# Both score banks awaited first, all four cross scores at once, and a re-ordered router in a two-layer decoder trunk

## What is computed

```python
def nsa(q, k, v):                     # 8 query heads, 2 key heads; two of its three branches are dense here
    s = q @ k.T * scale + t5_bias     # per head and branch: 256 tokens x 256 keys, causal
    return masked_softmax(s) @ v
...
def cross_attention(hn, memn, ...):   # 4 heads of 64
    s = jnp.einsum('bshd,bmhd->bhsm', q, k) * HEAD_DIM ** -0.5
    p = jax.nn.softmax(s, axis=-1)
    return jnp.einsum('bhsm,bmhd->bshd', p, v).reshape(bsz, seq, X_WIDTH) @ w_o
...
def moe_swiglu(x2, w_router, w_up, w_down):
    logits = x2 @ w_router
    top_val, top_idx = lax.top_k(logits, 2)
    gate = jax.nn.softmax(top_val, axis=-1)
    # each expert: gather its tokens, swiglu, times gate, add back
```

## Time and profile before

| what | value |
|---|---|
| time, median of 3 runs | 1373.01 us (1373.0 to 1373.81) |
| the profiled execution: its time | 1374.09 us |
| its span, first to last instruction | 1372.3 us |
| PE busy (x instructions) | 1310.5 us, 96% (x21428) |
| DVE busy | 636.4 us, 46% (x1404) |
| ACT busy | 425.5 us, 31% (x847) |
| mean granted clock of TensorE | 0.976 |
| experts, from their first up product to the end | 717.48 us to 1372.3 us |

### The profile page before, as it was taken

One profiled execution on the slowest core, in us unless ns is written; L12 is line 12 of the kernel. 1 busy time (PEld: TensorE's weight loads), 2 busy tenths in 40 slices (PEclk: granted clock), 3 DMA queues, 4 the chain that ended last, 5 costly groups with the idle time before them and its releaser, 6 DMA issues.

```text
span 1372.3 us, 48306 instructions
## 1 busy us (share of the span) xinstructions
PE 1310.5 (96%) x21428; PEld 1079.5 (79%) x21428; DVE 636.4 (46%) x1404; ACT 425.5 (31%) x847; POOL 89.8 (7%) x139
## 2 busy tenths in 40 slices
PE   7998897999999999989789999999999999999998
PEld 5855555777777685554659999999999999999997
DVE  7876313103322237651245555555555555455554
ACT  4425413001002122541313333343333333333332
POOL 0450100000000017000100000000000000000000
PEclk9997899999999999999889999999999999999999
DMA  8530043244241054102649999999999999999990
GB/s 351 211 123 1 1 184 122 90 171 184 104 172 62 34 240 154 63 1 90 248 175 390 426 426 427 426 427 426 426 426 427 427 426 426 427 426 426 426 403 33
DMA packets 32865, 357.68 MB, mean 261 GB/s; under 512 B 3715, under 2 KB 5379, under 8 KB 6700
## 3 DMA queue, kind: packets, MB, share of 16 engines
q1 hardware_dynamic: 30656, 353.78, 62.4%
q10 hardware_dynamic: 2156, 3.18, 0.7%
HBM read 355.88 MB, written 1.06 MB: 260 GB/s over the span
## 4 chain that ended last, share of the span: by engine, by line
PE 88%; DVE 5%; ACT 3%; issue 2%; DMA 1%; POOL 1%; ACTq 0%; POOLq 0%; DVEq 0%
PE bank L2102 29%; PE bank L1556 26%; PE bank L2118 14%; PE bank L2049 6%; PE bank L2164 2%; PE bank L2089 2%; PE bank L1564 1%; PE bank L1829 1%; PE bank L1706 1%; PE bank L1576 1%; PE bank L1894 1%; ACT ring L575 1%; DVE ring L968 1%; PE bank L1650 1%; PE bank L2002 0%
## 5 line engine op out<-in xcount | busy, mean ns | idle before, releaser
L2102 PE MATMUL bank<-R,ring 128*64 128x80 f32 x11264 | 421.7, 233 | 0.7 <-DVEq L950 0.7
L2102 PEld LDWEIGHTS bank<-R,ring 128*64 128x64 f32 x11264 | 403.0, 137 | 8.3 <-issue 8.3
L1556 PE MATMUL bank<-ring 128*128 128x256 f32 (+1 forms) x1408 | 368.4, 421 | 8.6 <-DVE ring L968 4.9
L1556 PEld LDWEIGHTS bank<-ring 128*128 128x128 f32 x1408 | 269.4, 193 | 106.2 <-issue 67.3
L841 ACT ACTIVATE ring<-ring 128x1024 f32<-128x1024 f32 x176 | 186.0, 1057 | 146.7 <-PE bank L2118 146.7
L2118 PE MATMUL bank<-zz,ring 128*64 128x80 f32 x5632 | 224.8, 233 | 0.0
L2118 PEld LDWEIGHTS bank<-zz,ring 128*64 128x64 f32 x5632 | 207.9, 137 | 0.0
L1518 DVE SCALAR_TENSOR_TENSOR zz<-zz,bank 128x80 f32<-128x80 f32 x176 | 41.9, 238 | 198.8 <-PE bank L2102 198.3
L1497 DVE COPY ring<-ring 128x1024 f32<-128x1024 f32 x177 | 121.6, 687 | 1.9 <-DVE R L1487 1.9
L1501 DVE COPY ring<-ring 128x1024 f32<-128x1024 f32 x177 | 121.5, 686 | 0.1
L837 ACT ACTIVATE X<-bank 128x80 f32<-128x80 f32 x176 | 41.7, 237 | 246.1 <-PE bank L2102 246.1
(11 more groups left out here) (299 smaller groups left out, 1029.4 us busy)
## 6 DMA issues: line engine op xcount, KB each, us to landing
ring<-moe_w_dram SPq DMA_DIRECT2D x177, 1536.0 KB, 10.7
ring<-ffn_w_dram SPq DMA_DIRECT2D x11, 3072.0 KB, 10.2
ring<-w_in_dram SPq DMA_DIRECT2D x6, 2048.0 KB, 10.4
ring<-w_out_dram SPq DMA_DIRECT2D x4, 2048.0 KB, 8.5
ring<-w_x_dram SPq DMA_DIRECT2D x2, 3072.0 KB, 10.6
ring<-w_small_dram SPq DMA_DIRECT2D x2, 2896.0 KB, 10.1
ring<-w_in_dram SPq DMA_DIRECT2D x2, 2144.0 KB, 21.0
ring<-bias_rows_dram ACTq DMA_DIRECT2D x1, 1536.0 KB, 11.1
```

The lines of the kernel that those rows point to most:

```text
L1556: i = pe.matmul(out_ap, a, b, start=(k == 0), stop=(k == n - 1))
L2102: e = pe.matmul(pb[out_bank][c0:c0 + 64, 0:CAP], half[:, P * k + c0:P * k + c0 + 64], xg[:, k], start=(k == 0), stop=(k == KT - 1), tile_p ...
```

## The change

Four things, all ahead of the experts. `scores(p)` opens both banks and then makes both products. The cross scores of units 0 to 3 go to banks 6, 7, 4 and 3 and are all made ahead of the first transposes; each unit has its own column of `nmx`, and DVE takes the four maxima without waiting for exponentials in between. In the router, the clearing of `table` and `zeros` stands ahead of the wait for the constants; the copies of the gates into `table` and the first step of `pos` stand ahead of the wait for `count`; the flag and the release of two banks (`overflow`) stand behind `pick(0)`. No instruction is added or left out.

```diff
@@ -44,6 +44,7 @@
 HEADS = [0, 4, 1, 5, 2, 6, 3, 7]
 SLOTS = 4
 BU_BANKS = [3, 4, 7, 1, 3, 4, 7, 3]
+XS_BANKS = [6, 7, 4, 3]
 S5_AT = [dict(bu0=4, bu4=7, bu6=9, ys0=10), dict(bu0=3, bu4=6, bu6=9, ys0=9)]
 UPW, DNW = KT * 2 * 256, 2 * D
 FF_SLOTS = [2, 3, 1, 0, 2, 3, 1, 0, 2, 3, 1]
@@ -213,7 +214,7 @@
             a(f"cross_T{g}_", g % 2)
         a("xq", 2, 2); a("xqT_", 3)
         for u in range(4):
-            a(f"xs{u}_", 6 + u % 2, 0)
+            a(f"xs{u}_", XS_BANKS[u], 0)
             a(f"xpT{u}_", u % 2)
         a("xo0_", 2); a("xo1_", 5); a("xoT", 3)
         for g in range(4):
@@ -570,10 +571,10 @@
                 act.activation(R[:, 0], turn_rows, ACT.Sin,
                                scale=-2 * math.pi, bias=cst[:, C_Q:C_Q + 1]).then_inc(sem["angles_ready"], 1)
 
-            def probs(buf, b, src, scale, to):
+            def probs(buf, b, src, scale, to, m):
 
                 return act.activation(s_of[buf][:, b * src.shape[-1]:(b + 1) * src.shape[-1]], src, ACT.Exp,
-                                      bias=nmx[:, buf, b:b + 1], scale=scale, accum_out=to)
+                                      bias=nmx[:, m, b:b + 1], scale=scale, accum_out=to)
 
             def pt_copy(buf, freed, name, n):
 
@@ -737,7 +738,7 @@
                     if v < 2 * NH:
                         act.wait_ge(sem["max_ready"], u + 1)
                         for b in range(2):
-                            e = probs(at(v), b, s_of[at(v)][:, b * nk:b * nk + nk], 1.0, sums[:, i, b, hh:hh + 1])
+                            e = probs(at(v), b, s_of[at(v)][:, b * nk:b * nk + nk], 1.0, sums[:, i, b, hh:hh + 1], at(v))
                         e.then_inc(sem["probs_ready"], 1)
                     if v == 1:
                         cmp_tanh()
@@ -802,7 +803,7 @@
                         banks.wait(act, f"xpT{k - 2}_{l}" if k >= 2 else f"pT1{NH - 2 + k}_{l}")
                         for b in range(2):
                             e = probs(k % 2, b, ps(f"xs{k}_{l}")[:, 256 * b:256 * b + 256], SCALE,
-                                      sums[:, i, 0, 2 * b + hp:2 * b + hp + 1])
+                                      sums[:, i, 0, 2 * b + hp:2 * b + hp + 1], k)
                         e.then_inc(sem["probs_ready"], 1)
                     if k:
                         pt_copy((k - 1) % 2, u - 2, f"xpT{k - 1}_{l}", 512)
@@ -1395,9 +1396,9 @@
                 for k in range(4):
                     u = 20 * l + 16 + k
                     banks.wait(dve, f"xs{k}_{l}")
-                    dve.wait_ge(sem["probs_ready"], u - 1)
-                    own(dve.tensor_reduce(nmx[:, u % 2], ps(f"xs{k}_{l}")[:].rearrange("p (b s) -> p b s", b=2), AX, ALU.max, negate=True))
-                    dve.tensor_scalar(nmx[:, u % 2], nmx[:, u % 2], SCALE, None, ALU.mult).then_inc(sem["max_ready"], 1)
+                    dve.wait_ge(sem["probs_ready"], 20 * l + 16)
+                    own(dve.tensor_reduce(nmx[:, k], ps(f"xs{k}_{l}")[:].rearrange("p (b s) -> p b s", b=2), AX, ALU.max, negate=True))
+                    dve.tensor_scalar(nmx[:, k], nmx[:, k], SCALE, None, ALU.mult).then_inc(sem["max_ready"], 1)
                 for i in range(NT):
                     dve.wait_ge(sem["probs_ready"], 20 * l + 18 + 2 * i)
                     own(dve.reciprocal(sumc[:, i, 0, 0:4], sums[:, i, 0, 0:4]))
@@ -1432,8 +1433,10 @@
                         dve.scalar_tensor_tensor(hT[:, t % 2], hT[:, 2 + t % 2], 0.5, up[:, 256:512], ALU.mult, ALU.mult).then_inc(sem["gated"], 1)
                     add_in("down")
 
+            own(dve.memset(table, 0.0))
+            own(dve.memset(zeros, 0.0))
+            dve.wait_ge(sem["moe_consts_loaded"], 16)
             banks.wait(dve, "router")
-            dve.wait_ge(sem["moe_consts_loaded"], 16)
             own(dve.tensor_copy(lg, ps("router")[:, 0:16].rearrange("p (i e) -> p i e", i=NT)))
             of_j = lg.unsqueeze(2).to_broadcast([P, NT, E, E])
             of_e = lg.unsqueeze(3).to_broadcast([P, NT, E, E])
@@ -1452,20 +1455,24 @@
             own(dve.tensor_reduce(gsum[:, 0:2], ex, AX, ALU.add))
             own(dve.reciprocal(gsum[:, 0:2], gsum[:, 0:2]))
             own(dve.tensor_tensor(ex, ex, spread(gsum[:, 0:2], [P, NT, E]), ALU.mult))
+            for i in range(NT):
+                own(dve.tensor_copy(table[:, 0:PASSES * E, 2 + i].rearrange("p (q e) -> p q e", e=E),
+                                    ex[:, i].unsqueeze(1).to_broadcast([P, PASSES, E])))
+            own(dve.tensor_scalar(pos, sel, -1e4, 1e4, ALU.mult, ALU.add))
 
             banks.wait(dve, "count")
-            own(dve.tensor_scalar(pos, sel, -1e4, 1e4, ALU.mult, ALU.add))
             own(dve.tensor_tensor(pos, pos, ps("count")[:, 0:16].rearrange("p (i e) -> p i e", i=NT), ALU.add))
-            own(dve.memset(table, 0.0))
+            passes = cste[:, C_PASS - C_MOE:C_PASS - C_MOE + PASSES * E].rearrange("p (q e) -> p q e", e=E)
             for i in range(NT):
-                own(dve.tensor_tensor(table[:, 0:PASSES * E, i].rearrange("p (q e) -> p q e", e=E), pos[:, i].unsqueeze(1).to_broadcast([P, PASSES, E]),
-                                      cste[:, C_PASS - C_MOE:C_PASS - C_MOE + PASSES * E].rearrange("p (q e) -> p q e", e=E), ALU.subtract))
-                own(dve.tensor_copy(table[:, 0:PASSES * E, 2 + i].rearrange("p (q e) -> p q e", e=E), ex[:, i].unsqueeze(1).to_broadcast([P, PASSES, E])))
-            own(dve.tensor_reduce(mx2[:, 2:3], ps("count")[:, 16:24], AX, ALU.max))
-            own(dve.tensor_scalar(flag[:, 0:1], mx2[0:1, 2:3], CAP + 0.5, None, ALU.is_gt))
-            signal(banks.drain("count"))
-            signal(banks.drain("router"))
-            signal(sem["flag_ready"])
+                own(dve.tensor_tensor(table[:, 0:PASSES * E, i].rearrange("p (q e) -> p q e", e=E),
+                                      pos[:, i].unsqueeze(1).to_broadcast([P, PASSES, E]), passes, ALU.subtract))
+
+            def overflow():
+                own(dve.tensor_reduce(mx2[:, 2:3], ps("count")[:, 16:24], AX, ALU.max))
+                own(dve.tensor_scalar(flag[:, 0:1], mx2[0:1, 2:3], CAP + 0.5, None, ALU.is_gt))
+                signal(banks.drain("count"))
+                signal(banks.drain("router"))
+                signal(sem["flag_ready"])
 
             def pick(e, wait_to):
 
@@ -1500,8 +1507,8 @@
                 expert_in(dve, turn, t)
                 dve.tensor_copy(st_value, hs[:, HS_ORDER[t % NHS], 1024:2048]).then_inc(sem["value_staged"], 1)
 
-            dve.memset(zeros, 0.0)
             pick(0, lambda k: dve.wait_ge(sem["e_step"], 1))
+            overflow()
             stage_gate(0, 0)
             for g in range(2):
                 gather_half("", g)
@@ -1823,9 +1830,10 @@
                     i, c = divmod(p, 4)
                     nk = P * (i + 1)
                     for g in range(2):
+                        banks.open(pe, f"sc{i}{2 * c + g}_{l}")
+                    for g in range(2):
                         nm = f"sc{i}{2 * c + g}_{l}"
                         rows = slice(HD * g, HD * g + HD)
-                        banks.open(pe, nm)
                         done(nm, pe.matmul(ps(nm)[:, 0:2 * nk].rearrange("p (b s) -> p b s", b=2), qT[rows, i, c], kT[rows, :, 0:nk],
                                            start=True, stop=True))
 
@@ -1993,6 +2001,7 @@
                 drained(f"mkT_{l}")
                 drained(f"xqT_{l}")
                 xscores(0)
+                xscores(1)
                 for k in range(4):
                     u = 20 * l + 16 + k
                     nm = f"xpT{k}_{l}"
@@ -2003,8 +2012,6 @@
                         if l == L - 1 and k == 2 and c == 0:
                             e.then_inc(sem["late0_read"], 1)
                     done(nm, e)
-                    if k == 1:
-                        xscores(1)
                     if k:
                         xvalues(k - 1)
                 xvalues(3)
```

## The result

| | before | after |
|---|---|---|
| time, median (lowest to highest) | 1373.01 us (1369.01 to 1373.81), 4 runs | 1357.95 us (1357.71 to 1360.56), 4 runs |
| the profiled execution: span | 1372.3 us | 1355.8 us |
| PE busy | 1310.5 us | 1291.7 us |
| mean granted clock | 0.976 | 0.984 |

The ratio is 0.9907, with a 95% interval of 0.9889 to 0.9926: 12.8 us faster (10.2 to 15.2). I had forecast 1367.7 us (1364.3 to 1371.0) and 5.3 us of gain.

The account below looks back on a forecast made before the run. The prediction took PE in the experts as the bound, so gains ahead arrive in full. Cross-attentions 2.6 + 2.4, router 1.2, pairs 0, clock -0.9 gave 5.3 us: 1373.0 - 5.3 = 1367.7 us, range 1364.3 to 1371.0.

Parts of the forecast that it names:

- The bound: Experts: PE is the bound and loads follow it, so gains ahead of them arrive at the end one to one.
- Rival C: Experts: loads at 426 GB/s are the bound, so time stays within 1 us of 1373; chance 0.05.
- Cross-attention: Both layers: making all scores first removes waits; gain 2.6 us (1.7 to 3.8) and 2.4 us (2.0 to 4.0).
- Router: Router: shorter DVE chain lets the first gather start earlier; gain 1.2 us (0.9 to 1.2).
- the end of the idle products as fixed: Ahead of the first gather: idle products end at 711.15, so PE can take all of the 1.19 us.
- The shift of `overflow`: Router: put behind the pick, it costs about 0.75 us, hidden by DVE's 1.90 us wait for the gather.
- Pairs of scores: Mixers: the second bank sets a pair's end, so opening both first is worth 0 (+0.1 to -0.1 each).
- -0.9 for the clock: Mixers: more idle PE ahead of split pairs keeps half clock for one more round; 0.9 us lost (0 to 7).
- four places of loss: Mixers, as rival: idle PE keeps half clock, 7.2 us lost, 1375.6 us; chance 0.10 for same, 0.04 for slower.
- Rival B: Cross-attentions and first gather at full clock: 11.2 us gained, 1361.8 us; chance 0.10 for it or halfway to it.
- halfway to B: Lower end of the forecast range, halfway to Rival B, given as 1364.3 us.
- half of the gain eaten: Upper end of the forecast range: half clock behind split pairs eats half of the gain, given as 1371.0 us.

Follow-up runs that it names:

- e11: Kernel before, with 3, 8 and 5 idle products behind units 5, 9 and 13 of each mixer; 1358.57 us, ratio 0.9916.
- e2: Kernel before, with only the cross-attention part of the change; 1365.45 us, ratio 0.9951.
- e1: Kernel before, with only both score banks opened ahead of both products of a pair; 1368.04 us, ratio 0.9976.
- e8: Kernel before, with seven idle products behind the first scores of each cross-attention; 1372.54 us, ratio 1.0007.
- e6: Changed kernel, but in calls 2, 3 and 6 of each layer the pair's second product waits for the first; 1370.19 us, ratio 0.9991.
- e7: Changed kernel, with 3, 8 and 5 idle products behind units 5, 9 and 13 of each mixer; 1349.67 us, ratio 0.9845.
- e10: Changed kernel, with the idle mixer products of e7 and without the four idle products ahead of the first gather; 1353.27 us, ratio 0.9878.

## Why the prediction was wrong, point by point

**The bound.** Right: 649.9 us of experts before and after, so what was gained ahead arrived at the end. Rival C is out for a gain of this size.

**Cross-attention.** Mechanism right, size off. I booked 2.6 and 2.4. All eight traces with the new order take 20.3 us in both layers, 3.7 and 5.0 less than the profiled before. The order is worth 2.3 a layer (e11, first layer), near my terms. What I sized wrongly was the clock: I kept the half clock of before for the four pieces, and with the new order neither stage has any, which gave 1.4 and 2.7 on top.

**Router.** 1.2 us, right at a given clock: 4.98 us from the logits' copy to the pick where the old order took 6.28 and 6.04, and at half clock 5.82 where e2 with the old order took 7.05. But I took the end of the idle products as fixed. At half clock they end later, and the gather waits 1.0 us longer behind the pick (2.04 against 1.08). The other 2.2 us between the two profiled executions are not the change's: the four other traces with the old router (e1, e2, e8, e11) take 21.0 to 22.5 there, not 24.5. In the profiled execution of before the constants were late, and the gather ran at half clock. The shift of `overflow` was hidden, as said.

**Pairs of scores: the step that failed.** I wrote "each is worth 0. I take 0", then set -0.9 for the clock, and as a rival four places of loss. The end of a pair is indeed unmoved, but the clock term has the wrong sign: in place of the 0.9 us lost, 3.3 us were gained alone (e1), and about 3.6 on top of the other parts by the ratios (0.9914 against 0.9940, on two chips), because the first mixer has 14 to 17 us at half clock instead of 24 to 27. I took idle time as what decides; it did grow, from 2.91 to 4.93 us, and the half clock fell. e6 keeps that idle time and only runs the products one after the other, and the half-clock stretches are back, also where the clock fell at the same moment as in e1. So in this kernel it is the two products running at once that brings the clock back sooner. I also counted six split pairs where there were eight. The Trainium skill ("TensorEngine Tiling (Array Packing)", Key Properties) says that tiles work in parallel; I had set that rule aside as it did not move the end of a pair. The traces agree with the rule (2.08 us at once, 4.17 one after the other, both at half clock), and what I missed is what it does to the clock. Why the clock comes back sooner, the runs do not show.

**Rival B** (the clock gives more) came in at both cross-attentions. The gather ran at full clock too (2.44 us instead of 4.39), but it did so in e1, e8 and e11 with the old router as well, so its half clock in the profiled execution of before was chance and none of it is the change's. Its price, 1361.8, missed the mixers.

**Sum by the runs.** Pairs 3.3, cross 6.7, router 0.5: 10.5 us, where the whole measured 12.8 and 11.8 (0.9907 and 0.9914). The difference is within the intervals of the parts, 1.4, 2.3 and 1.8 us. I had set the measurement's own spread too low besides: 23 runs of the kernel before on one chip go from 1368.94 to 1375.38, and they follow the mean granted clock (1368.9 to 1370.4 us at 0.980, 1372.9 to 1375.4 at 0.973 and 0.972). The ends of my range were loosely set as well: halfway to B is 1364.8 and not 1364.3, half of the gain eaten is 1370.4 and not 1371.0. Neither reaches the measured time.

## What to carry to other kernels

Where a small product is at half clock in the trace, price each edit twice, by its order and by what it does to the clock; here the second was more than half of the gain (3.3 us in the mixers, 1.4 and 2.7 in the cross-attentions), and in the mixers it came although the ends of the pairs did not move. Two products that use different parts of the array were better released together here, even though the first had to wait for it; try it where a trace shows such a pair split. And the cheapest test of how much the clock holds is to fill PE's waits with idle products: 16 a layer took a further 9.2 us off. They are not free everywhere: the seven of e8 cost 0.5 us in a cross-attention that was at full clock.

## What the runs showed of the hardware that I had not expected

The clock came back sooner when two products ran at once behind 4.93 us of idle PE than when the first ran early behind 2.91: 4.0 us after the start of the pair of call 6 in the first layer, instead of 9.7. The Trainium skill ("TensorE: Matmul & The Clock Gate", What's actually happening) has the throttle released by activity; e7 agrees, with a granted clock of 1.00 in the first mixer.

In all three kernels with idle products in the mixers, PE stood still at the same place far behind them, at its entry into the loop of steps in the first expert, without a wait that the profile shows ("issue"): 1.84 us in e7, 2.60 in e10, 2.08 in e11. In the others it did not, or for 0.46 (e2). The timelines of e10

```profile
695.31 0.44 PE L2158 MATMUL bank<-R 1*128 1x320 bf16 x2
698.36 2.15 PE L2113 MATMUL bank<-R,ring 128*64 128x80 f32 x32 [2.60 <-issue]
```

and of the changed kernel's second run, at the same place:

```profile
703.84 0.44 PE L2154 MATMUL bank<-R 1*128 1x320 bf16 x2
704.22 1.33 PE L2109 MATMUL bank<-R,ring 128*64 128x80 f32 x32
```

With the half clock that follows it in e10 and e11, the experts take 651.8 (e7), 654.2 (e10) and 653.7 us (e11) instead of 649.9; 2.4 us of e10's loss against e7 lie here. No wait for the loads of weights is in these rows.

The traces also record the transfers of instructions. In each of the four kernels where PE stood still, a transfer of 16 KB of instructions began 2.6 to 2.9 us before PE went on: at 693.18 us in e7 (PE goes on at 696.06), 695.54 in e10 (698.36), 701.08 in e11 (703.67), 708.36 in e2 (711.01). In the nine others it began 3.1 to 5.1 us before PE came to this place, and PE did not stop. So the wait fits one for instructions; this rests on times alone, no edit tried it, and why the transfer begins late in these four stays open.
